# An RWKV-7 chunk inverse on 32x32 diagonal blocks instead of 64x64 ones

## The reference

```
def _rwkv7_step(state, inp):
    r_t, w_t, k_t, v_t, a_t, b_t = inp
    sa = jnp.einsum('bhvk,bhk->bhv', state, a_t)
    state = (state * w_t[:, :, None, :] + sa[..., None] * b_t[:, :, None, :]
             + v_t[..., None] * k_t[:, :, None, :])
    return state, jnp.einsum('bhvk,bhk->bhv', state, r_t)
...
    _, ys = lax.scan(_rwkv7_step, state0, xs)
```

## Time and profile before

| | |
|---|---|
| median of 3 runs | 1341.08 us |
| profiled execution, its own time | 1335.52 us |
| its span | 1333.7 us |
| TensorE matmul busy | 1201.3 us (90%) |
| VectorE busy | 737.7 us (55%) |
| inverse of t=0, from its second X2 to its last dY | 28.4 us (991.15 to 1019.55) |
| inverse of t=1, with scan and moments | 42.95 us (1040.50 to 1083.45) |
| mean granted clock of TensorE | 0.967 |

### The profile page before, as it was taken

One profiled execution on the slowest core, in us unless ns is written; L12 is line 12 of the kernel. 1 busy time (PEld: TensorE's weight loads), 2 busy tenths in 40 slices (PEclk: granted clock), 3 DMA queues, 4 the chain that ended last, 5 costly groups with the idle time before them and its releaser, 6 DMA issues.

```text
span 1333.7 us, 20901 instructions
## 1 busy us (share of the span) xinstructions
PE 1201.3 (90%) x9007; PEld 860.1 (64%) x9007; DVE 737.7 (55%) x1189; ACT 246.7 (18%) x426; POOL 93.4 (7%) x86
## 2 busy tenths in 40 slices
PE   5999999899784778996999999899999879999997
PEld 4855644556342433785478888676769774788886
DVE  5547412133221114726487777677876648777774
ACT  5413211120010004413110000325421110100000
POOL 2010000010000000210000000000110531000000
PEclk9999999989987888988999999999999999999999
DMA  9553245086999999330765561334200216755500
GB/s 346 196 184 126 65 153 223 0 351 271 420 421 415 422 420 376 115 124 1 258 216 188 189 189 63 95 126 164 81 2 4 88 45 231 243 189 181 182 17 31
DMA packets 106484, 247.27 MB, mean 185 GB/s; under 512 B 8130, under 2 KB 56273, under 8 KB 93971
## 3 DMA queue, kind: packets, MB, share of 16 engines
q1 hardware_dynamic: 106196, 245.71, 50.4%
q0 software_dynamic: 144, 0.15, 0.0%
q10 hardware_dynamic: 46, 0.01, 0.0%
HBM read 244.80 MB, written 1.05 MB: 184 GB/s over the span
## 4 chain that ended last, share of the span: by engine, by line
PE 75%; DMA 9%; DVE 9%; ACT 3%; SPq 2%; issue 2%; POOL 1%; DVEq 0%
PE bank L483 13%; PE bank L482 13%; PE bank L484 13%; PE bank L345 8%; PE bank L331 6%; DMA work<-expert_w_gate 5%; PE bank L2402 4%; PE bank L1342 3%; DMA work<-expert_w_down 2%; PE bank L1357 2%; SPq L301 2%; DMA ring_w<-expert_w_gate 1%; PE bank L1393 1%; PE bank L445 1%; PE bank L1084 1%
## 5 line engine op out<-in xcount | busy, mean ns | idle before, releaser
L482 PE MATMUL bank<-work_rounded,work_rounded 128*128 128x512 f32 (+2 forms) x704 | 278.7, 396 | 6.8 <-DVE work_rounded L1716 5.2
L484 PE MATMUL bank<-work_rounded,work_rounded 128*128 128x512 f32 (+2 forms) x704 | 274.9, 391 | 0.0
L483 PE MATMUL bank<-ring_w_rounded,work_rounded 128*128 128x512 f32 (+2 forms) x576 | 227.1, 394 | 0.0
L482 PEld LDWEIGHTS bank<-work_rounded,work_rounded 128*128 128x128 f32 x704 | 133.5, 190 | 37.4 <-issue 3.9
L484 PEld LDWEIGHTS bank<-work_rounded,work_rounded 128*128 128x128 f32 x704 | 133.1, 189 | 28.4
L483 PEld LDWEIGHTS bank<-ring_w_rounded,work_rounded 128*128 128x128 f32 x576 | 109.6, 190 | 23.0 <-issue 0.2
L345 PE MATMUL bank<-ring_w,work 128*128 128x512 f32 x256 | 112.1, 594 | 3.1 <-ACT work L1147 1.4
L1716 DVE TENSOR_TENSOR ring_w_rounded<-ring_w,work_rounded 128x1024 fp32r<-128x1024 f32 x84 | 102.9, 1225 | 2.9
L1240 ACT ACTIVATE work<-bank 128x256 f32<-128x256 f32 x52 | 20.0, 386 | 424.2 <-PE bank L484 340.3
L345 PEld LDWEIGHTS bank<-ring_w,work 128*128 128x128 f32 x256 | 47.8, 190 | 60.7 <-issue 56.6
L331 PE MATMUL bank<-ring_w,work 128*128 128x512 f32 x192 | 83.5, 593 | 0.9 <-DVE work L455 0.9
(11 more groups left out here) (446 smaller groups left out, 1827.7 us busy)
## 6 DMA issues: line engine op xcount, KB each, us to landing
ring_w<-ffn_w_down SPq DMA_DIRECT2D x22, 1024.0 KB, 5.2
ring_w<-expert_w_gate SPq DMA_DIRECT2D x16, 1024.0 KB, 17.1
ring_w<-expert_w_up SPq DMA_DIRECT2D x16, 1024.0 KB, 21.9
work<-expert_w_down SPq DMA_DIRECT2D x16, 1024.0 KB, 26.7
work<-expert_w_up SPq DMA_DIRECT2D x13, 1024.0 KB, 21.6
ring_w<-expert_w_down SPq DMA_DIRECT2D x12, 1024.0 KB, 25.9
work<-ffn_w_gate SPq DMA_DIRECT2D x12, 1024.0 KB, 5.5
work<-ffn_w_up SPq DMA_DIRECT2D x12, 1024.0 KB, 8.1
```

What stands on the lines that cost most here:

```text
L482: nc.tensor.matmul(out, lhsT[0], rhs[0], start=first, stop=False)
L483: nc.tensor.matmul(out, lhsT[0], rhs[1], start=False, stop=False)
L484: return nc.tensor.matmul(out, lhsT[1], rhs[0], start=False, stop=last)
```

## The change

The levels work on the 32x32 diagonal blocks of the 64x64 matrices. A tile has four of them per head, one on each quarter of the partitions (`QUARTER`). `Xs`, `Ys` and `PM` hold 32 columns per head where `Xi`, `Yi` and `PM` held 64. Four levels take the blocks from 2 to 32. A group (`quarters_pe`) is 32 matmuls of 32x32x32 instead of 16 of 64x64x64. `join_pe` then computes the missing off-diagonal quarter of the 64x64 inverse from the two 32x32 ones in two further rounds (Pj, then Yj), and `join_dve` writes `Yi` from them. `products_dve` folds the two column halves of the 2x2 start into `Ys`.

```
-        LEVELS = 5
+        QUARTER = [slice(SB * g, SB * (g + 1)) for g in range(P // SB)]
+        LEVELS = 4
...
-                blocks_pe(pe, "A", "X2", t, half, lambda w, h: Yi[t][w, h], lambda w, h: C("eye2")[w])
+                quarters_pe(pe, "A", "X2", t, half, lambda g, h: Ys[QUARTER[g], h], lambda g, h: C("eye4")[QUARTER[g]])
+
+        def quarters_pe(pe, ring, name, t, half, lhs, rhs):
+
+            ps = fill(pe, ring, f"{name}.{t}.{half}")
+            for h in range(8):
+                for g, own in enumerate(QUARTER):
+                    mm = nc.tensor.matmul(ps[own, h * SB:(h + 1) * SB], lhs(g, 8 * half + h), rhs(g, 8 * half + h),
+                                          start=True, stop=True)
+            mm.then_inc(full[ring], 1)
...
-                blocks_pe(pe, "D", f"P{lv}", t, half, lambda w, h: NM[t][w, h, 0:CH], lambda w, h: Xi[w, h])
+                quarters_pe(pe, "D", f"P{lv}", t, half, lambda g, h: NM[t][QUARTER[g], h, SB * (g % 2):SB * (g % 2 + 1)],
+                            lambda g, h: Xs[QUARTER[g], h])
...
-                if lv < LEVELS - 1:
-                    blocks_pe(pe, "D", f"dX{lv}", t, half, lambda w, h: Yi[t][w, h], lambda w, h: PM[w, h])
-                blocks_pe(pe, "D", f"dY{lv}", t, half, lambda w, h: PM[w, h], lambda w, h: Yi[t][w, h])
+                quarters_pe(pe, "D", f"dX{lv}", t, half, lambda g, h: Ys[QUARTER[g], h], lambda g, h: PM[QUARTER[g], h])
+                quarters_pe(pe, "D", f"dY{lv}", t, half, lambda g, h: PM[QUARTER[g], h], lambda g, h: Ys[QUARTER[g], h])
+
+        def join_pe(pe, t):
+
+            first = lambda g: QUARTER[g - g % 2]
+            second = lambda g: QUARTER[g - g % 2 + 1]
+            for half in range(2):
+                await_moved(pe, f"dX{LEVELS - 1}.{t}.{half}")
+                quarters_pe(pe, "D", "Pj", t, half, lambda g, h: NM[t][first(g), h, SB:CH], lambda g, h: Xs[first(g), h])
+            for half in range(2):
+                await_moved(pe, f"Pj.{t}.{half}", f"dY{LEVELS - 1}.{t}.{half}")
+                quarters_pe(pe, "D", "Yj", t, half, lambda g, h: C("eye4")[second(g)] if g % 2 else PM[second(g), h],
+                            lambda g, h: Ys[second(g), h])
...
-                V.tensor_tensor(Yi[t][:, h8], Yi[t][:, h8], bc(C("eye2"), 8, 1), ALU.add).then_inc(sem("Y2"), 1)
+                links["dve"](V.tensor_tensor(Ys[:, h8], Yi[t][:, h8, 0:SB], Yi[t][:, h8, SB:CH], ALU.add))
+                V.tensor_tensor(Ys[:, h8], Ys[:, h8], bc(C("eye4"), 8, 1), ALU.add).then_inc(sem("Y2"), 1)
...
-                    V.tensor_tensor(Xi[:, h8], Xi[:, h8], eight(ps), ALU.add).then_inc(moved["D"], 1)
+                V.tensor_tensor(Xs[:, h8], Xs[:, h8], quarter(ps), ALU.add).then_inc(moved["D"], 1)
...
+        def join_dve(dve, t):
+            V = nc.vector
+            for half in range(2):
+                h8 = slice(8 * half, 8 * half + 8)
+                ps = take(dve, "D", f"Pj.{t}.{half}")
+                V.tensor_copy(PM[:, h8], quarter(ps)).then_inc(moved["D"], 1)
+            for half in range(2):
+                h8 = slice(8 * half, 8 * half + 8)
+                await_moved(dve, f"dY{LEVELS - 1}.{t}.{half}")
+                V.tensor_scalar(Yi[t][:, h8, 0:SB], Ys[:, h8], C("even"), None, ALU.mult)
+                ps = take(dve, "D", f"Yj.{t}.{half}")
+                V.tensor_copy(Yi[t][:, h8, SB:CH], quarter(ps)).then_inc(moved["D"], 1)
```

More of the change, by code:

```diff
@@ L38 @@
 CH = 64
+SB = CH // 2
 GL, DL = 160, 64
@@ L94, in _constants, with below @@
     parts["eye2"] = np.concatenate([np.eye(CH)] * 2, 0)
[L95 to L104, removed]
+    def below(n, b):
+        i_, j_ = np.arange(n)[:, None], np.arange(n)[None, :]
+        return (i_ // (2 * b) == j_ // (2 * b)) & ((i_ // b) % 2 == 1) & ((j_ // b) % 2 == 0)
+    levels = [below(SB, b) for b in (2, 4, 8, 16)]
+    parts["rwlev"] = np.concatenate([np.concatenate(levels, 1)] * (P // SB), 0).astype(float)
+    parts["rwlevT"] = np.concatenate([below(CH, 1).T] * 2, 0).astype(float)
+    parts["eye4"] = np.concatenate([np.eye(SB)] * (P // SB), 0)
+    parts["even"] = ((i // SB) % 2 == 0).astype(float)[:, None]
     parts["strictP"] = (i[:, None] < i[None, :]).astype(float)
@@ L2186, in build @@
         MV = [R0[:, 2048:3072].rearrange("p (h n) -> p h n", h=RH), view(2048, RH, HD)]
-        Xi = RB[:, 0:1024].rearrange("p (h n) -> p h n", h=RH)
+        Xs = RB[:, 0:512].rearrange("p (h n) -> p h n", h=RH)
+        Ys = RB[:, 512:1024].rearrange("p (h n) -> p h n", h=RH)
         Yi = [RB[:, 1024 * (1 + t):1024 * (2 + t)].rearrange("p (h n) -> p h n", h=RH) for t in range(T)]
-        PM = RB[:, 3072:4096].rearrange("p (h n) -> p h n", h=RH)
+        PM = RB[:, 3072:3584].rearrange("p (h n) -> p h n", h=RH)
         UG = RB[:, 4096:6144].rearrange("p (h n) -> p h n", h=RH)
@@ L2344, in rwkv_pe @@
                 level_pe(pe, 0, lv)
+            join_pe(pe, 0)
             turn_pe(pe, 1)
@@ L2352, in rwkv_pe @@
                     scan_pe(pe, 1)
+            join_pe(pe, 1)
             chunks_pe(pe, 1)
@@ L2429, in chunks_pe @@
             for half in range(2):
-                await_moved(pe, f"dY{LEVELS - 1}.{t}.{half}", f"Mv.{t}.{half}")
+                await_moved(pe, f"Yj.{t}.{half}", f"Mv.{t}.{half}")
                 for g in (2 * half, 2 * half + 1):
@@ L2580, in inverse_start_act @@
             for half in range(2):
-                for name, to in (("Mv", MV[t]), ("X2", Xi)):
+                for name, to in (("Mv", MV[t]), ("X2", Xs)):
                     ps = take(act, "A", f"{name}.{t}.{half}")
-                    nc.scalar.copy(flat(to[:, 8 * half:8 * half + 8]), ps[:, :]).then_inc(moved["A"], 1)
+                    to = flat(to[:, 8 * half:8 * half + 8])
+                    nc.scalar.copy(to, ps[:, 0:to.shape[1]]).then_inc(moved["A"], 1)
         def chunks_act(act, t):
@@ L2717, in rwkv_dve @@
                 level_dve(dve, 0, lv)
+            join_dve(dve, 0)
             products_dve(dve, 1)
@@ L2728, in rwkv_dve @@
                     variance_dve(dve, 0)
+            join_dve(dve, 1)
             chunks_dve(dve, 1)
@@ L2767, in products_dve @@
                 links["dve"](V.tensor_tensor(Yi[t][:, h8], NM[t][:, h8, 0:CH], bc(C("rwlevT"), 8, 1), ALU.mult))
-                V.tensor_tensor(Yi[t][:, h8], Yi[t][:, h8], bc(C("eye2"), 8, 1), ALU.add).then_inc(sem("Y2"), 1)
+                links["dve"](V.tensor_tensor(Ys[:, h8], Yi[t][:, h8, 0:SB], Yi[t][:, h8, SB:CH], ALU.add))
+                V.tensor_tensor(Ys[:, h8], Ys[:, h8], bc(C("eye4"), 8, 1), ALU.add).then_inc(sem("Y2"), 1)
+        quarter = lambda ps: ps[:, 0:8 * SB].rearrange("p (h n) -> p h n", h=8)
         def level_dve(dve, t, lv):
@@ L2773, in level_dve @@
                 ps = take(dve, "D", f"P{lv}.{t}.{half}")
-                V.tensor_tensor(PM[:, 8 * half:8 * half + 8], eight(ps), bc(C("rwlev")[:, lv * CH:(lv + 1) * CH], 8, 1),
+                V.tensor_tensor(PM[:, 8 * half:8 * half + 8], quarter(ps), bc(C("rwlev")[:, lv * SB:(lv + 1) * SB], 8, 1),
                                 ALU.mult).then_inc(moved["D"], 1)
@@ L2777, in level_dve @@
                 h8 = slice(8 * half, 8 * half + 8)
[L2778 to L2781, removed]
-                    V.tensor_tensor(Xi[:, h8], Xi[:, h8], eight(ps), ALU.add).then_inc(moved["D"], 1)
-                ps = take(dve, "D", f"dY{lv}.{t}.{half}")
-                V.tensor_tensor(Yi[t][:, h8], Yi[t][:, h8], eight(ps), ALU.add).then_inc(moved["D"], 1)
+                ps = take(dve, "D", f"dX{lv}.{t}.{half}")
+                if lv == 0:
+                    await_moved(dve, f"X2.{t}.{half}")
+                V.tensor_tensor(Xs[:, h8], Xs[:, h8], quarter(ps), ALU.add).then_inc(moved["D"], 1)
+                ps = take(dve, "D", f"dY{lv}.{t}.{half}")
+                V.tensor_tensor(Ys[:, h8], Ys[:, h8], quarter(ps), ALU.add).then_inc(moved["D"], 1)
+        def join_dve(dve, t):
[10 more added lines that the diff above has]
+                V.tensor_copy(Yi[t][:, h8, SB:CH], quarter(ps)).then_inc(moved["D"], 1)
         def chunks_dve(dve, t):
```

## The result

| | before | after |
|---|---|---|
| median | 1339.74 us (4 runs) | **1385.51 us** (1383.29 to 1386.38, 4 runs) |
| profiled execution, its span | 1335.52, 1333.7 us | 1385.49, 1383.7 us |
| mean granted clock | 0.967 | 0.931 |

The account below looks back on a forecast made before the run. TensorE was taken as the bound, just above its program's arrival rate, 3.67 us per 256 instructions. t=0 +24.8 and t=1 +23.7 sum to 48.5, taken as +48 on 1341.08: 1389 us, range 1368 to 1402.

Parts of the forecast that it names:

- The program arrives in blocks of 256 instructions: TensorE's instruction queue: 3.67 us per block, TensorE idle for "issue" between blocks, 89 packets instead of 74.
- below one half: Sign in the levels (line 2423): TensorE's busy share in the stage falls below one half.
- t=0, 53.2 us, +24.8: Inverse of the first 128 tokens: 14.5 blocks at 3.67 us, 53.2 us instead of 28.4.
- A group takes the array 0.93 us or less: Array time of a 32x32 group on TensorE, hidden behind the 1.84 us in which its 128 instructions arrive.
- VectorE hidden at 0.42 us a result: VectorE in the levels: 0.42 us per result instead of 0.69, hidden behind a group every 1.84 us.
- Between, 0, within 2: Transposes, products and chunks of t=0, between the two inverses: same instructions, 0 us, within 2 either way.
- t=1, 66.6 us, +23.7: Inverse of the second 128 tokens: 15.5 blocks, 56.9 us, plus 9.7 for loads, instead of 42.9 us.
- the price of the loads: Four 1 MB loads of w_ro during t=1, each delaying a program block: 4 x 2.4 = 9.7 us.
- After, 0: Chunks, scan and output of t=1, behind its inverse: unchanged, 0 us.
- A: Rival in the inverses: fetch is no wall, VectorE sets the pace, 11 us less per tile, 1319 us; chance 0.07.
- B: Rival in the inverses: fetch reserve covers half the extra instructions, or groups cost 0.93 us; no change, 1341 us; chance 0.05.
- C: Rival on TensorE's array: four tiles overlap no better than two, 29.2 ns a record, +27 us per tile, 1395 us; chance 0.06.

Follow-up runs that it names:

- half: Changed kernel with half the matmuls per group, each moving two heads' columns (64), second head's own block left out: 1330.54 us, ratio 0.9973.
- aturn: Changed kernel with X as VectorE's block transpose of Y, X2 and dX gone from TensorE: 1352.67 us, ratio 1.0133.
- wide: Changed kernel with the same matmuls of 32x32 tiles, but 64 moving columns each instead of 32: 1386.33 us, ratio 1.0365.
- late: Changed kernel with the four 1 MB loads of w_ro held back until the join of t=1 is done: 1389.19 us, ratio 1.0385.
- dup: Kernel before with a matmul of one moving column ahead of each X2 or level matmul: 1418.38 us, ratio 1.0614.
- lean: Kernel before with levels of 32 columns per head on 64x64 tiles, X by VectorE's transpose, X2 and dX gone: 1348.09 us, ratio 1.0055.
- pad: Kernel before with four long-satisfied semaphore waits ahead of each X2 or level matmul: 1510.77 us, ratio 1.1272.
- lean64: lean with each matmul moving its 32 columns twice, 64 columns in all: 1320.11 us, ratio 0.9877.

## Why the prediction was right

1389 was predicted (1368 to 1402), 1385.51 measured; against the profiled executions +48 was predicted and +50.0 measured.

- *The program arrives in blocks of 256 instructions.* Right: breaks ahead of every 127 or 128 MATMUL, starts 3.55 to 3.97 us apart (mean 3.68, taken were 3.67), 89 packets, busy share just over a half (28.35 of 53.4, where "below one half" was said; the clock at half speed lengthened the runs between the breaks). half and aturn show that the number of instructions, and wide that neither columns nor clock, sets the pace. What in the delivery of a block takes this long stays open: the DMA engines are busy 2% of the time in t=0.
- *t=0, 53.2 us, +24.8.* Measured 53.4, +25.0.
- *A group takes the array 0.93 us or less.* Right: counted as in the prediction (less the 0.22 us that a record is shown long), 128 records, two groups, take 1.82 us at a clock of 0.50, 0.91 a group; at full clock the row below shows 62 in 0.52 us, 8.4 ns each, 0.54 us a group. It is hidden in both cases.

```profile
989.13 0.74 PE L2423 MATMUL bank<-const,ring_w 32*32 32x32 f32 x62 [0.50 <-DVE ring_w L2797]
```

- *VectorE hidden at 0.42 us a result.* Right.
- *Between, 0, within 2.* Too low: 24.80 instead of 20.95 us, **+3.85**. This is the first term that was mis-sized. The stage opens with the same 32 transposes, in the changed kernel at a granted clock of 0.64 over them (0.50 up to 1046), in the kernel before at 1.00 (after, then before):

```profile
1042.56 5.66 PE L2382 MATMUL bank<-const,work 128*128 128x128 f32 x32
```

```profile
1019.46 3.71 PE L2378 MATMUL bank<-const,work 128*128 128x128 f32 x32
```

  That is 1.95 us. The two breaks towards its end are longer by 1.37 us together, 1.46 and 0.96 where they were 0.35 and 0.70 (start and length in the chain):

```profile
1061.13 1.46 issue
...
1065.38 0.96 issue
```

  That the stage begins without a block in hand would explain these; this was argued, not tested, and the last 0.5 us stay open.
- *t=1, 66.6 us, +23.7.* Measured 63.25, **+20.3**. The term that failed is the price of the loads, 4 x 2.4 = 9.7 us, taken from two single breaks. By late they cost 4.4 us in all, less than half of the term; without them the stage is 58.9, 2 us above the 56.9 of the sum.
- *After, 0.* 253.15 instead of 250.25 us, **+2.9**: the clock is still 0.52 for the first 5 us, which was priced (5 us with the one between), but at the high end alone.

The start of t=0 was 2.05 us earlier than before, nothing the change touches. 25.0 + 3.85 + 20.3 + 2.9 - 2.05 = 50.0. So the mechanism and the term of t=0 were right, and that the whole came within 2 us is in part luck: loads 5.3 us too dear stood against a clock left out of the sum and a stage between that was taken as nothing.

- *Rivals.* A (1319, no wall): refuted by the breaks. B: refuted, the two inverses cost 45.3 us more and not nothing. C (tiles don't overlap, a record keeps 29.2 ns): refuted here, since four 32x32 tiles give a record per 8.4 ns at full clock; but its price per record is real for two tiles, as dup showed.

The prediction read the kernel before as bound by TensorE, just above the rate of its program. Both hold, and more evenly than it said: half, with 16 us of TensorE's time in t=0 where the kernel before has 28, gains at most 0.5%, so the two walls are equally high.

The Trainium skill (Runtime: NRT & Kernel Launch, Instruction fetch mechanics) calls the fetch hidden by the slower sequencer; 42.3 us of idle time on one line, and half, say otherwise for tiny matmuls.

## What to carry to other kernels

Cutting small matmuls into smaller ones that run side by side can win array time and still lose: count TensorE's instructions (four per fp32 matmul here) and hold 3.7 us per 256, 3.68 to 3.85 on average in these runs, against the time in which the array uses them. A row of idle time marked "issue", with 256 instructions from one to the next, is that wall already in sight. Where the wall bound, fewer instructions were what helped here: a transpose by VectorE in place of groups of matmuls (aturn), and more moving columns per matmul (half). Read the granted clock beside it: lean had 20 packets fewer than the changed kernel and still lost to the array at half clock.

## What the runs showed of the hardware

TensorE's granted clock stands at one of two levels in these traces, 0.50 or 1.00 (1.2 or 2.4 GHz); a figure between them is a stretch with both. In the changed kernel it was 1.00 in the row of 62 records shown above, 0.50 from 994.46 on, and rose after 1046, under the 32 transposes. Over the levels of t=0 it was 0.53 in the changed kernel (32 moving columns, TensorE busy 53%) and 0.50 in lean (32 columns, busy all the time), but 1.00 in half (64 columns, busy 58%), 0.94 in wide and 0.95 in lean64 (64 columns). The changed kernel and wide, and lean and lean64, differ on TensorE in the moving columns alone. That isn't all that counts: pad, with 64 columns, shown busy but with a record only every 123 ns, had 0.52, and dup, with one and 64 columns in turn, 1.00 in t=0 and 0.69 over t=1. No rule follows from these runs. Behind a wall of program half clock cost little (wide gained nothing by it in the whole); where the array was the bound it cost 25 to 28 us (lean against lean64).

A load of 1 MB beside the arriving program delayed it by 1.1 us on average (late), with 1 to 2 us of chance in the 4.4 for the four, where two single breaks had suggested 1.8 and 3.1. Behind the stage the same four loads cost 4.85 us.
